# Strassen blocks with 512-column passes over both halves of the input, modulation sums stacked before one turn

## The chip, the cores and the metric

The kernel runs on one core of a Trainium2 chip. The metric is the time of one execution on the device in microseconds. The engines are named as the profile names them: PE (TensorE, its weight loads as PEld), DVE (VectorE), ACT (ScalarE), POOL (GpSimd) and SP (SyncE, which issues most transfers).

## The reference

Two transformer blocks in float32 on 512 tokens of width 1024. What this change touches is the feed-forward part of each block and the modulation of the second one:

```
h = rmsnorm(x, ...)                              # (512, 1024)
y = (silu(h @ w_gate) * (h @ w_up)) @ w_down     # hidden width 2816, once in each block

mod = silu(c) @ mod_w + mod_b                    # c (1, 1024), mod_w (1024, 6144), second block only
shift1, scale1, gate1, shift2, scale2, gate2 = split(mod, 6)
```

## The kernel before

Every large product is computed in three passes of fp32r matmuls. Weight and input are split into a high part (ACT casts it) and a low part (DVE subtracts), and PE adds hi x hi, hi x lo and lo x hi in PSUM. A unit of weights is 1024 rows by 256 columns (or 512 by 512) and is loaded by SP into one of two `raw` slots; the slots of `w_hi` and `w_lo` alternate too. PSUM is `bank`, 8 banks of 512 columns.

**Up stage.** There are two of them (`hidden` on ACT and DVE, `blocks` on POOL and PE), with `which` 0 and 1. The first 4 of 22 units are plain. The other 18 are *blocks* m = 0 to 17: one block holds the same 128 columns of gate and up, and is computed by a Strassen scheme with 7 products of a quarter of the weights (4 k-tiles of 128 rows) and 256 tokens, 12 matmuls of 256 columns each. PE takes them in the order P7, P6, P4 of block m, P1 of block m+1, P5 of m, P2 of m+1, P3 of m (`pe_order`, and the loop at L2437). P1, P6, P5 and P3 add up in one region "x"; P2, P7 and P4 have a region each, half a bank wide (`region`, L628).

Around the products, block m needs on DVE, in this order: `pair_lo` of m+1 (L1748), the product of m-1 (L1814), `b22_lo` (L1771, its end lets SP load the weights of block m+2), two sums of weight quarters of m+1, t1 and t3 (L1735, L1741), z = P6 + P7 (L1831), c21 = z - P4 (L1834), `sums_lo` of m+1 (L1757), c22 (L1840), `t4_lo` and `t1_lo` of m+1 (L1764 twice), the last product (L1845), and the sum with P2 of m+1 (L1820). POOL makes t2 (L987, after t1) and t4 (L991, after t2) of block m+1. ACT casts the high parts and copies P7 (L1264) and P1 (L1233) out of PSUM. `sums_lo` reads t2, so it waits for POOL; PE waits for c22 of m before P3 of m, and for `sums_lo` of m+1 before P7 of m+1. Each engine runs its list strictly in order; all waits are on counters whose values follow from these lists (`dve_order`, `act_order`, `wait_pool`).

**Modulation.** For the four early pairs of 1024 columns, DVE multiplies slabs of `mod_w` with silu(c) and adds them, over 128 partitions (`early_slab`), into one of two accumulators. For each pair PE then turns the accumulator with 8 transposes (`mod_columns`, L2589) and DVE sums the turned columns (L1702): twice in the k stage and twice in the va stage. The gate of the last norm is spread over the partitions by 4 matmuls (`mod_gate` on PE, L2596 and L2597) in the second down stage; its high part is cast by ACT (`mod_hi_part(5)`) in that stage, and its low part is made by POOL (`mod_lo_part(5)`, L1052) after the last block.

Of the kernel before, what the change touches and what calls it, by code (L numbers as in the profile page):

```python
# [31 lines left out]
F32 = mybir.dt.float32  # L32
# [5 lines left out]
P = 128  # L38
# [105 lines left out]
def build(nc, a, out):  # L144
    with ExitStack() as ctx:
# [15 lines left out]
        h_hi = at("h_hi", 48, [P, KD, TOK], F32R)  # L161
        h_lo = at("h_lo", 64, [P, KD, TOK], F32R)
# [42 lines left out]
        s_hi = at("s_hi", A + 12, [P, 4, 4, 256], F32R)  # L205
        s_lo = at("s_lo", A + 28, [P, 4, 4, 256], F32R)
# [249 lines left out]
        class Chain:  # L456
# [46 lines left out]
        GAINS_READY, GATE_READY = {1: 5, 2: 7}, {2: 8, 3: 9}  # L503
# [158 lines left out]
        def dve_order():  # L662
# [3 lines left out]
            for m in range(BLOCKS):  # L666
# [6 lines left out]
                yield from [f"sums {ahead}"] if ahead else []  # L673
                yield f"c22 {m}"
                yield from [f"t4 {ahead}", f"t1_lo {ahead}"] if ahead else []
# [24 lines left out]
        def wait_pool(eng, which, m, total):  # L700


            eng.wait_ge(block_pool, 2 * BLOCKS * which + 2 * m + total)
# [178 lines left out]
        def _(gp):  # L882
# [54 lines left out]
            def early_pairs():  # L937

                for e, pair in enumerate(EARLY):
                    acc, col = mod_both[e % 2], 512 * MOD_PAIRS[pair][0]  # L940
                    wait(gp, mod_read, e - 1)
# [13 lines left out]
            def mod_pair(pair):  # L955

                place = LATER.index(pair)
                wait(gp, mod_read, len(EARLY) + place)
# [20 lines left out]

            def blocks(n0, which):  # L980

                for m in range(BLOCKS):
# [8 lines left out]
                    gp.tensor_tensor(t4, t2, quarter_of(n, 1, 0), ALU.subtract).then_inc(block_pool, 1)  # L991

# [4 lines left out]
            gp.wait_ge(mod_read, 3)  # L997
# [72 lines left out]
        def _(act):  # L1070
# [48 lines left out]
            def post_norm(k, n0, units, xn, gain, shift):  # L1119
# [6 lines left out]
                for j in range(units):  # L1126
# [4 lines left out]
                    if k == 3 and j == 1:  # L1131
                        mod_hi_part(5)
# [1814 lines left out]
```

## Time and profile before

| | |
|---|---|
| median of 3 runs (lowest, highest) | 1534.05 us (1533.6, 1534.14) |
| the profiled execution's own time | 1534.35 us |
| its span, from the first to the last instruction | 1532.6 us |
| granted clock of TensorE over the span | 0.999 of 2.4 GHz |
| first up stage, blocks 0 to 17 | from 471.15 to 654.07 us |
| second up stage, blocks 0 to 17 | from 1222.28 to 1405.20 us |
| share of the chain that ended last | PE 96%, DVE 2%, ACT 1% |

A matmul's duration in the profile holds its way through the array, and matmuls overlap; what one costs in a stream is the distance between two starts. The same holds, less strongly, for DVE and ACT, where the next instruction starts a little before the one ahead has ended.

### The profile page before, as it was taken

The numbers are of one execution on the slowest core, as the hardware profiler recorded it, in microseconds if no ns is written. First come the engines' busy times: TensorE is split into PE (matmuls) and PEld (weight loads), VectorE is DVE, ScalarE is ACT, GpSimd is POOL, SyncE is SP. The second block draws the span as 40 slices with busy tenths as digits, with TensorE's granted clock in tenths as the row PEclk, the third lists the DMA queues.
The fourth block names the chain that finished last, engine by engine and source line by source line (L and its number), as shares of the span: only waits on it lengthen the run. The fifth ranks groups of instructions, "written<-read, shape, count | busy, mean of one in ns | idle before, by whom it ended". The sixth has DMA issues, their size and how long they took to land.

```text
span 1532.6 us, 23103 instructions
## 1 busy us (share of the span) xinstructions
PE 1521.0 (99%) x8916; PEld 1340.0 (87%) x8916; DVE 989.4 (65%) x1427; ACT 675.3 (44%) x1109; POOL 386.5 (25%) x350
## 2 busy tenths in 40 slices
PE   9999999999999999999999999999999999999998
PEld 9888887888899999988898888888888999999886
DVE  4776667547588777773276979644456977777323
ACT  5223444423454544442186775332226554455221
POOL 3211004210112222396010802692012122222000
PEclk9999999999999999999999999999999999999999
DMA  7875113322432444354222211453232233334231
GB/s 214 301 256 165 56 55 69 111 83 83 137 108 59 110 111 110 114 189 144 91 84 69 83 55 57 136 154 114 90 101 65 83 110 106 93 106 143 91 110 55
DMA packets 188726, 171.41 MB, mean 112 GB/s; under 512 B 19793, under 2 KB 161105, under 8 KB 188625
## 3 DMA queue, kind: packets, MB, share of 16 engines
q1 hardware_dynamic: 181456, 144.84, 31.5%
q0 software_dynamic: 7168, 25.19, 5.0%
q8 instruction: 68, 1.11, 0.3%
q14 instruction: 34, 0.27, 0.1%
HBM read 167.91 MB, written 2.10 MB: 111 GB/s over the span
## 4 chain that ended last, share of the span: by engine, by line
PE 96%; DVE 2%; ACT 1%; issue 0%; POOL 0%; DMA 0%; SPq 0%; DVEq 0%; ACTq 0%; POOLq 0%
PE bank L2321 19%; PE bank L2323 19%; PE bank L2322 19%; PE bank L2415 7%; PE bank L2417 7%; PE bank L2416 7%; PE bank L2480 2%; PE bank L2481 2%; PE bank L2484 2%; PE bank L2644 1%; PE bank L2376 1%; PE bank L2389 1%; PE bank L2385 1%; PE bank L2543 1%; PE bank L2655 1%
## 5 line engine op out<-in xcount | busy, mean ns | idle before, releaser
L1572 DVE TENSOR_TENSOR w_lo<-raw,w_hi 128x2048 fp32r<-128x2048 f32 (+1 forms) x109 | 213.3, 1958 | 216.9 <-ACT w_hi L1082 216.6
L2321 PE MATMUL bank<-h_hi,w_hi 128*128 128x512 f32 (+1 forms) x800 | 308.9, 386 | 0.0
L2323 PE MATMUL bank<-h_hi,w_lo 128*128 128x512 f32 (+1 forms) x800 | 298.5, 373 | 0.0
L2322 PE MATMUL bank<-h_lo,w_hi 128*128 128x512 f32 (+1 forms) x800 | 298.2, 373 | 0.0
L1082 ACT CAST w_hi<-raw 128x2048 fp32r<-128x2048 f32 (+1 forms) x108 | 171.5, 1588 | 200.1 <-PE bank L2323 194.1
L2321 PEld LDWEIGHTS bank<-h_hi,w_hi 128*128 128x128 f32 x800 | 150.9, 189 | 28.5 <-issue 1.9
L2322 PEld LDWEIGHTS bank<-h_lo,w_hi 128*128 128x128 f32 x800 | 151.0, 189 | 27.0 <-issue 1.9
L2323 PEld LDWEIGHTS bank<-h_hi,w_lo 128*128 128x128 f32 x800 | 150.7, 188 | 27.1
L2415 PE MATMUL bank<-s_hi,w_hi 128*128 128x256 f32 x576 | 163.4, 284 | 2.0 <-DVE act_m L1840 2.0
L2417 PE MATMUL bank<-s_hi,w_lo 128*128 128x256 f32 x576 | 163.0, 283 | 0.0
L2416 PE MATMUL bank<-s_lo,w_hi 128*128 128x256 f32 x576 | 163.0, 283 | 0.0
L987 POOL TENSOR_TENSOR w_sum<-raw,act_m 128x512 f32<-128x512 f32 x36 | 48.9, 1358 | 314.4 <-PE bank L2417 225.6
L2416 PE MATMUL bank<-h_lo,w_hi 128*128 128x256 f32 x432 | 122.3, 283 | 0.0
L2417 PE MATMUL bank<-h_hi,w_lo 128*128 128x256 f32 x432 | 122.2, 283 | 0.0
L2415 PE MATMUL bank<-h_hi,w_hi 128*128 128x256 f32 x432 | 122.2, 283 | 0.0
L2415 PEld LDWEIGHTS bank<-s_hi,w_hi 128*128 128x128 f32 x576 | 110.5, 192 | 2.8 <-DVE act_m L1840 2.8
L2416 PEld LDWEIGHTS bank<-s_lo,w_hi 128*128 128x128 f32 x576 | 110.6, 192 | 0.0
L2417 PEld LDWEIGHTS bank<-s_hi,w_lo 128*128 128x128 f32 x576 | 110.6, 192 | 0.0
L2321 PE MATMUL bank<-w_hi,act_hi 128*128 128x512 f32 x280 | 109.0, 389 | 0.0
L2323 PE MATMUL bank<-w_hi,act_lo 128*128 128x512 f32 x280 | 108.9, 389 | 0.0
L2322 PE MATMUL bank<-w_lo,act_hi 128*128 128x512 f32 x280 | 108.9, 389 | 0.0
L2415 PEld LDWEIGHTS bank<-h_hi,w_hi 128*128 128x128 f32 x432 | 82.9, 192 | 0.1
(489 smaller groups left out, 3217.8 us busy)
## 6 DMA issues: line engine op xcount, KB each, us to landing
raw<-in_w_in SPq DMA_DIRECT2D x102, 512.0 KB, 4.6
raw<-in_w_ffn_in SPq DMA_DIRECT2D x44, 512.0 KB, 5.1
mod_slabs<-in_mod_w POOLq DMA_DIRECT2D x16, 1024.0 KB, 6.0
raw<-in_w_gate SPq DMA_DIRECT2D x22, 512.0 KB, 4.0
raw<-in_w_up SPq DMA_DIRECT2D x22, 512.0 KB, 5.2
raw<-in_w_down SPq DMA_DIRECT2D x20, 512.0 KB, 4.6
raw<-in_w_ffn_out SPq DMA_DIRECT2D x20, 512.0 KB, 4.4
mod_raw<-in_mod_w POOLq DMA_DIRECT2D x32, 256.0 KB, 3.1
```

The costliest lines, as they stand in the source:

```text
L987: gp.tensor_tensor(t2, quarter_of(n, 1, 1), four(t1_sum(m)), ALU.subtract).then_inc(block_pool, 1)
L1082: ins = act.copy(w_hi[s][:, cols], raw[s][:, cols])
L1572: ins = dve.tensor_tensor(w_lo[s][:, cols], raw[s][:, cols], w_hi[s][:, cols].bitcast(F32), ALU.subtract)
L2321: pe.matmul(o, st_hi, mv_hi, start=first, stop=False)
L2322: pe.matmul(o, st_hi, mv_lo, start=False, stop=False)
L2323: return pe.matmul(o, st_lo, mv_hi, start=False, stop=last)
L2415: pe.matmul(o, hi[:, k, :], mv_hi(k), start=first and k == 0, stop=False, skip_group_check=not first)
L2416: pe.matmul(o, hi[:, k, :], mv_lo(k), start=False, stop=False, skip_group_check=not first)
L2417: ins = pe.matmul(o, lo[:, k, :], mv_hi(k), start=False, stop=k == 3, skip_group_check=not first)
L2480: pe.matmul(bank[:, t, 0:width], x_hi[:, k0 + k, ts], hi[:, k, :], start=first and k == 0, stop=False)
L2481: pe.matmul(bank[:, t, 0:width], x_lo[:, k0 + k, ts], hi[:, k, :], start=False, stop=False)
L2484: ins = pe.matmul(bank[:, t, 0:width], x_hi[:, k0 + k, ts], lo[:, k, :], start=False, stop=last and k == kt - 1)
```

## The change

P2, P7 and P4 no longer run hi x hi and hi x lo as two matmuls of 256 columns. The high and low parts of the input lie in one tensor (`h_parts`, `s_parts`), and one matmul of 512 columns takes both (two stretches of 256, 16 KB apart); its results lie side by side in one bank, hi x lo in the second half (`both_parts`). Lo x hi stays a matmul of 256 columns into the first half. All 8 banks are used, 4 for even and 4 for odd blocks. The second halves are added afterwards: those of P2 and P4 by one more DVE instruction each (L1856 and L1869 of the changed kernel), that of P7 by ACT, which copies both halves, and POOL, which adds them (L1009); z waits for POOL.

The products on PE:

```diff
                     for k in range(4):
+                        parts = moving(k)
+                        if name == "x":
+                            pe.matmul(o, hi[:, k, :], parts[:, 0, :], start=first and k == 0, stop=False, skip_group_check=not first)
+                            pe.matmul(o, hi[:, k, :], parts[:, 1, :], start=False, stop=False, skip_group_check=not first)
+                        else:
+                            pe.matmul(both_parts(m, name), hi[:, k, :], parts, start=k == 0, stop=k == 3, skip_group_check=True)
+                        ins = pe.matmul(o, lo[:, k, :], parts[:, 0, :], start=False, stop=k == 3,
+                                        skip_group_check=not first or name != "x")
```

ACT's copies of P7, and behind t2 and t4 of the same block POOL's sum:

```diff
-                    act.copy(act_m[:, PLAIN + m, 256:512], region(m, "p7")).then_inc(block_act, 1)
+                    act.copy(act_m[:, PLAIN + m, 256:512], region(m, "p7"))
+                    act.copy(act_m[:, PLAIN + m, 0:256], region(m, "p7", 1)).then_inc(block_act, 1)
...
+                    if which == 1 and m == 4:
+                        mod_lo_part(5)
+                    wait_act(gp, which, f"p7 {m}")
+                    p7, p7_second = act_m[:, PLAIN + m, 256:512], act_m[:, PLAIN + m, 0:256]
+                    gp.tensor_tensor(p7, p7, p7_second, ALU.add).then_inc(block_pool, 1)
```

DVE in block m:

```diff
-                    dve.tensor_tensor(g[:, 0:256], region(m, "p2"), g[:, 0:256], ALU.add)
+                    chain.mark(dve.tensor_tensor(g[:, 0:256], region(m, "p2"), g[:, 0:256], ALU.add))
                     if m + 1 < BLOCKS:
                         pair_lo(m + 1)
+                    chain.wait()
+                    dve.tensor_tensor(g[:, 0:256], region(m, "p2", 1), g[:, 0:256], ALU.add)
...
-                    wait_act(dve, which, f"p7 {m}")
+                    wait_pool(dve, which, m, 3)
...
-                    dve.tensor_tensor(g[:, 256:512], g[:, 256:512], region(m, "p4"), ALU.subtract).then_inc(block_dve, 1)
-                    if m + 1 < BLOCKS:
+                    then(dve.tensor_tensor(g[:, 256:512], g[:, 256:512], region(m, "p4"), ALU.subtract))
+                    dve.tensor_tensor(g[:, 256:512], g[:, 256:512], region(m, "p4", 1), ALU.subtract).then_inc(block_dve, 1)
+                    if 0 < m < BLOCKS - 1:
                         sums_lo(m + 1)
...
                     dve.tensor_tensor(mid[:, 256:512], region(m, "x"), mid[:, 256:512], ALU.add).then_inc(block_dve, 1)
+                    if m == 0:
+                        sums_lo(1)
```

In the first block c22 stands ahead of `sums_lo(1)`. In the last block PE has one set of transposes (first up stage) or the gate's 4 matmuls (second) between P5 and P3. ACT's cast for that gate moves into block 1 of the second stage and POOL's low part into block 4.

```diff
+                    else:
+                        wait_dve(pe, which, f"c21 {m}")
+                        if which == 0:
+                            mod_columns(0)
+                        else:
+                            mod_gate(5, 6)
                     wait_dve(pe, which, f"c22 {m}")
```

The four early accumulators are not turned one by one. DVE folds each from 128 to 32 partitions and stacks the four in `mod_acc`; PE turns the stack once, in the last block of the first up stage; DVE sums 32 columns at a time (`early_columns`, two reductions) after that stage.

```diff
+            def fold(e):
+                acc = mod_both[e % 2][:].rearrange("p a n -> p (a n)")
+                stack = mod_stack[:].rearrange("p a n -> p (a n)")
+                dve.wait_ge(mod_summed, SLABS * (e + 1))
+                then(dve.tensor_tensor(acc[0:64, :], acc[0:64, :], acc[64:128, :], ALU.add))
+                dve.tensor_tensor(stack[32 * e:32 * e + 32, :], acc[0:32, :], acc[32:64, :], ALU.add).then_inc(mod_out, 1)
...
-                mod_columns(i, (shift_col[0], gain_sums[0])[i])
+                fold(i)
```

How the lists of the engines change shows in three places. First DVE, one block in the middle of the first up stage, before (from `pair_lo` of m+1 on):

```order
L1748 TENSOR_TENSOR w_lo_53<-raw_50,w_hi_51 128x1024
L1814 TENSOR_TENSOR act_m<-bank,silu_t 128x256
L1771 TENSOR_TENSOR w_lo_54<-raw_49,w_hi_52 128x512
L1735 TENSOR_TENSOR act_m<-raw_50 128x512
L1741 TENSOR_TENSOR w_sum_87<-raw_50 128x512
L1831 TENSOR_TENSOR silu_t<-bank,act_m 128x256
L1834 TENSOR_TENSOR silu_t<-silu_t,bank 128x256
L1757 TENSOR_TENSOR w_lo_53<-w_sum_87,w_hi_51 128x1024
L1840 TENSOR_TENSOR act_m<-bank,act_m 128x256
```

The same stretch of DVE in the changed kernel (line numbers are its own):

```order
L1780 TENSOR_TENSOR w_lo_53<-raw_50,w_hi_51 128x1024
L1856 TENSOR_TENSOR silu_t<-bank,silu_t 128x256
L1846 TENSOR_TENSOR act_m<-bank,silu_t 128x256
L1803 TENSOR_TENSOR w_lo_54<-raw_49,w_hi_52 128x512
L1767 TENSOR_TENSOR act_m<-raw_50 128x512
L1773 TENSOR_TENSOR w_sum_86<-raw_50 128x512
L1865 TENSOR_TENSOR silu_t<-bank,act_m 128x256
L1868 TENSOR_TENSOR silu_t<-silu_t,bank 128x256
L1869 TENSOR_TENSOR silu_t<-silu_t,bank 128x256
L1789 TENSOR_TENSOR w_lo_53<-w_sum_86,w_hi_51 128x1024
L1875 TENSOR_TENSOR act_m<-bank,act_m 128x256
```

L1856 (second half of P2) stands ahead of the product and of `b22_lo`, L1869 (second half of P4) ahead of `sums_lo`; nothing has left the list.

POOL, before, the end of the second up stage (L987 is t2, L991 is t4):

```order
L991 TENSOR_TENSOR w_sum_87<-w_sum_88,raw_50 128x512
L987 TENSOR_TENSOR w_sum_88<-raw_49,act_m 128x512
L991 TENSOR_TENSOR w_sum_87<-w_sum_88,raw_49 128x512
L1052 TENSOR_TENSOR mod_lo<-mod_acc,mod_hi 128x1024
L895 TENSOR_SCALAR sq_y<-sq_y 128x1
```

POOL in the changed kernel, blocks 3 to 5 of the second up stage (L1000 is t2, L1004 is t4, L1009 the new sum of P7's halves, L991 the gate's low part):

```order
L1000 TENSOR_TENSOR w_sum_87<-raw_49,act_m 128x512
L1004 TENSOR_TENSOR w_sum_86<-w_sum_87,raw_49 128x512
L1009 TENSOR_TENSOR act_m<-act_m 128x256
L1000 TENSOR_TENSOR w_sum_87<-raw_50,act_m 128x512
L1004 TENSOR_TENSOR w_sum_86<-w_sum_87,raw_50 128x512
L991 TENSOR_TENSOR mod_lo<-mod_acc,mod_hi 128x1024
L1009 TENSOR_TENSOR act_m<-act_m 128x256
```

Every block's sum stands between t4 of this block and t2 of the next; the gate's low part, 1024 columns, has come forward from behind the last block to right behind t4 of block 4.

## Rows read from the trace of the kernel before

**Rows 1.** The page's part 1: busy us of each engine, share, instructions.
```profile
PE 1521.0 (99%) x8916; PEld 1340.0 (87%) x8916; DVE 989.4 (65%) x1427; ACT 675.3 (44%) x1109; POOL 386.5 (25%) x350
```

**Rows 2.** Waits of PE: line, releaser, total us, times, longest.
```profile
PE bank L2415 <- DVE act_m L1840: 2.0, 4, 0.6
```

**Rows 3.** Timeline of PE in the blocks: start, duration, line, operation, idle.
```profile
484.00 0.28 PE L2415 MATMUL bank<-s_hi,w_hi 128*128 128x256 f32 x1
...
490.49 0.28 PE L2415 MATMUL bank<-s_hi,w_hi 128*128 128x256 f32 x1
...
563.92 0.28 PE L2415 MATMUL bank<-s_hi,w_hi 128*128 128x256 f32 x1
```

**Rows 4.** Timeline of PE: the waits in the first and last block.
```profile
483.19 0.39 PE L2415 MATMUL bank<-s_hi,w_hi 128*128 128x256 f32 x1 [0.36 <-DVE act_m L1840]
...
652.54 0.39 PE L2415 MATMUL bank<-s_hi,w_hi 128*128 128x256 f32 x1 [0.62 <-DVE act_m L1840]
```

**Rows 5.** Timeline of PE: one set of columns, one gate, what follows.
```profile
101.99 1.04 PE L2589 MATMUL bank<-ident,mod_acc 128*128 128x128 f32 x8
102.78 0.47 PE L2576 MATMUL bank<-h_hi,wf_both 128*40 128x512 f32 x1
...
1443.31 0.39 PE L2596 MATMUL bank<-mod_hi,ones_r 128*128 128x512 f32 x1
...
1444.22 0.39 PE L2480 MATMUL bank<-w_hi,act_hi 128*128 128x512 f32 x1
```

**Rows 6.** Timeline of DVE, blocks 1 and 2 of the first stage.
```profile
477.59 0.69 DVE L1735 TENSOR_TENSOR act_m<-raw 128x512 f32<-128x512 f32 x1
...
484.59 0.42 DVE L1820 TENSOR_TENSOR silu_t<-bank,silu_t 128x256 f32<-128x256 f32 x1
485.34 1.23 DVE L1748 TENSOR_TENSOR w_lo<-raw,w_hi 128x1024 fp32r<-128x1024 f32 x1 [0.33 <-ACT w_hi L1201]
...
487.41 0.68 DVE L1735 TENSOR_TENSOR act_m<-raw 128x512 f32<-128x512 f32 x1
...
492.54 0.42 DVE L1840 TENSOR_TENSOR act_m<-bank,act_m 128x256 f32<-128x256 f32 x1
```

**Rows 7.** Timeline of DVE, a block in the middle.
```profile
557.28 0.69 DVE L1735 TENSOR_TENSOR act_m<-raw 128x512 f32<-128x512 f32 x1
...
561.31 1.22 DVE L1757 TENSOR_TENSOR w_lo<-w_sum,w_hi 128x1024 fp32r<-128x1024 f32 x1 [1.01 <-POOL w_sum L991]
562.68 0.43 DVE L1840 TENSOR_TENSOR act_m<-bank,act_m 128x256 f32<-128x256 f32 x1
```

**Rows 8.** Timeline of POOL.
```profile
23.45 0.21 POOL L912 TENSOR_TENSOR start_sel<-ident 128x8 fp32r<-128x8 f32 x1
...
478.35 1.68 POOL L987 TENSOR_TENSOR w_sum<-raw,act_m 128x512 f32<-128x512 f32 x1 [13.84 <-DVE act_m L1735]
...
558.48 1.29 POOL L987 TENSOR_TENSOR w_sum<-raw,act_m 128x512 f32<-128x512 f32 x1 [7.35 <-PE bank L2417]
559.91 1.30 POOL L991 TENSOR_TENSOR w_sum<-w_sum,raw 128x512 f32<-128x512 f32 x1
...
1135.12 2.40 POOL L1052 TENSOR_TENSOR mod_lo<-mod_acc,mod_hi 128x1024 fp32r<-128x1024 f32 x1 [89.17 <-ACT mod_hi L1117]
```

**Rows 9.** Timeline of DVE and POOL in the first down stage.
```profile
656.28 2.62 DVE L1572 TENSOR_TENSOR w_lo<-raw,w_hi 128x2048 fp32r<-128x2048 f32 x1
...
657.72 2.33 POOL L973 TENSOR_TENSOR mod_acc<-mod_acc,mod_raw 128x512 f32<-128x512 f32 x1
...
658.82 1.77 DVE L1714 TENSOR_TENSOR act_lo<-act_m,act_hi 128x512 fp32r<-128x512 f32 x1
```

**Rows 10.** Timeline of ACT.
```profile
484.25 1.05 ACT L1201 CAST w_hi<-raw 128x1024 fp32r<-128x1024 f32 x1 [1.27 <-DMA raw<-in_w_up]
...
556.92 0.37 ACT L1264 COPY act_m<-bank 128x256 f32<-128x256 f32 x1 [0.82 <-PE bank L2417]
...
1234.77 1.05 ACT L1201 CAST w_hi<-raw 128x1024 fp32r<-128x1024 f32 x1 [0.66 <-DMA raw<-in_w_ffn_in]
```

More of the change, by code:

```diff
@@ L672, in dve_order @@
                 yield f"c21 {m}"
-                yield from [f"sums {ahead}"] if ahead else []
+                yield from [f"sums {ahead}"] if ahead and m > 0 else []
                 yield f"c22 {m}"
+                yield from [f"sums {ahead}"] if m == 0 else []
                 yield from [f"t4 {ahead}", f"t1_lo {ahead}"] if ahead else []
@@ L957, in mod_pair @@
                 place = LATER.index(pair)
-                wait(gp, mod_read, len(EARLY) + place)
+                gp.wait_ge(mod_read, 1 + place)
                 then(gp.memset(mod_acc[:], 0.0))
@@ L1270, in hidden @@
                     act.activation(g, g, ACT.Silu).then_inc(block_act, 1)
+                    if which == 1 and m == 1:
+                        mod_hi_part(5)
                     if m + 1 < BLOCKS:
@@ L1910, in _ @@
             early_slab(12)
-            mod_columns(2, gain_sums[1])
+            fold(2)
             early_slab(13)
@@ L2408, in blocks, with product @@
             def blocks(n0, which):
-                def product(m, i, name, mv_hi, mv_lo, first=True):
+                def product(m, i, name, moving, first=True):
                     hi, lo, o = four(operand(w_hi, n0, i)), four(operand(w_lo, n0, i)), region(m, name)
                     for k in range(4):
-                        pe.matmul(o, hi[:, k, :], mv_hi(k), start=first and k == 0, stop=False, skip_group_check=not first)
-                        pe.matmul(o, hi[:, k, :], mv_lo(k), start=False, stop=False, skip_group_check=not first)
-                        ins = pe.matmul(o, lo[:, k, :], mv_hi(k), start=False, stop=k == 3, skip_group_check=not first)
+                        parts = moving(k)
[6 more added lines that the diff above has]
+                                        skip_group_check=not first or name != "x")
                     ins.then_inc(product_done, 1)
@@ L2580, in mod_columns @@
             def mod_columns(place):
-                early = place < len(EARLY)
-                acc = mod_both[place % 2] if early else mod_acc
-                pe.wait_ge(mod_summed, SLABS * (place + 1) if early else SLABS * len(EARLY) + 1)
-                wait(pe, mod_out, place if early else 0)
+                if place == 0:
+                    pe.wait_ge(mod_out, len(EARLY))
+                else:
+                    pe.wait_ge(mod_summed, SLABS * len(EARLY) + 1)
+                acc = (mod_stack, mod_acc)[place]
                 for q in range(KD):
@@ L2609, in _ @@
             f_pairs(n_q + 2, 1)
-            for i in range(2):
-                for j in range(2):
-                    for f in range(2):
-                        feature_tile(n_k + j, f, pair_pace(i))
-                mod_columns(i)
+            f_pairs(n_k, 2)
             pe.wait_ge(wf_split, 2)
@@ L2619, in _ @@
                 for j in range(2):
[L2620 to L2626 removed]
+                    token_unit(n_va + j, h_hi, h_lo, 4 * j, j == 0, j == 1, chunk_pace(c))
                     if c != j:
                         pe.wait_ge(rows_split, 1)
[L2629 removed]
                         for h in range(4 * c, 4 * c + 4):
```

117 lines of the change are left out of this document (58 added, 59 removed).

## The prediction

> **What bounds the kernel now.** The page's busy times come first: PE works 1521.0 of 1532.6 us, DVE two thirds of that [rows 1]. Then PE's waits: nearly the only ones it has in the up stages are four for c22 (L1840 of DVE), 2.0 us together [rows 2]. So in the blocks PE is the bound, and what a matmul costs there is the distance of starts: from 484.00 to 490.49 us lie 54 matmuls of 256 columns, 0.120 us each [rows 3]. For 512 columns the gate's four give (1444.22 - 1443.31) / 4 = 0.2275 us [rows 5]. A block of 84 matmuls takes 84 x 0.120 = 10.08 us. The third view asks how near the others are behind PE. In the middle of a stage c22 starts at 562.68 and lasts 0.43, and P3, which waits for it, starts at 563.92 [rows 3, 7]: it is ready 0.8 us early. The fourth view is the order of work: in a block DVE, then POOL, then DVE again make one ring, and this ring decides the case.
>
> **The ring, before.** t1 (DVE) -> t3 -> t2, t4 (POOL) -> `sums_lo` -> c22 -> `t4_lo`, `t1_lo` -> last product -> P2's sum -> `pair_lo` -> product -> `b22_lo` -> t1 of the next block. Where nothing but itself held it, at the start of the first stage, t1 starts at 477.59 and 487.41 [rows 6], 9.82 us. In it DVE stood still before `pair_lo`, whose weights came late [rows 10]: P2's sum starts at 484.59 and an instruction of this kind frees DVE after 0.33 (its 0.42 less the overlap), so 485.34 - 484.92 = 0.42 us. The ring by itself takes 9.40 us, 0.68 less than PE's block.
>
> **PE's saving.** In each block 3 products x 4 tiles lose one matmul: 2 x 0.120 - 0.2275 = 0.0129 us, 0.155 a block, 5.6 us for 36 blocks. PE's block falls to 9.93 us, if nothing else holds it. No row has a matmul that reads two stretches; the bounds are 0.2275 and 0.240 (two matmuls of 256), and I take the former. The Trainium skill (TensorE: Matmul & The Clock Gate, Back-to-back issue gap) gives an isolated gap of N / 2.4 + 2.5 ns. By it a removed matmul would save 2.5 ns, an estimate of 1.1 us in all; the rows' distances hold 13 ns above N / 2.4, so here the trace decides.
>
> **What is added to the ring.** First P2's second half (L1856 after), one more PSUM instruction of 256 columns: 0.33 us; it also stands ahead of `b22_lo`. Second POOL's sum of P7's halves. P4's second half (0.5 us with the wait for the first) falls into the 1.0 us that DVE waits for POOL before `sums_lo` [rows 7], and is free. POOL's instruction: 8 columns took 0.21, 1024 columns 2.40, 512 columns 1.29 [rows 8], a line of 0.19 + 2.16 ns a column, so 0.74 us for 256. Bounds: 0.65 (half of 1.29) and 1.29 (no faster than 512 columns); I take the line.
>
> When does it run? ACT's copy of P7 starts 0.2 us after P7's end (556.92 [rows 10]), takes 0.26 for each half, so POOL may start about 2.3 us after P7's start. DVE is then in `b22_lo`, with t1 and t3 right behind. All three read two SBUF operands, and there the trace shows that DVE and POOL keep each other out. t2 at 478.35, begun while t3 ran, took 1.68 us, and 1.29 at 558.48 when t3 had just ended [rows 8]. In the down stage a POOL sum begun at 657.72, in the middle of a DVE subtraction, took 2.33 instead of 1.29, and DVE's next one, from 658.82, took 1.77 instead of 0.69, ending 0.54 after POOL's [rows 9]. So at the end of a DVE instruction the waiting POOL gets in, and DVE waits until 0.15 us before POOL's end. This is what the Trainium skill states (SBUF — State Buffer, SBUF: two separate sides): one port pair is shared as an exclusive lock, for a DVE instruction with two SBUF inputs against a GpSimd instruction that reads SBUF; the trace agrees. Hence POOL's sum holds t1 up by 0.74 - 0.15 = 0.59, less what it can overlap with the end of `b22_lo`: 0.52. The sum lies ahead of t2 in POOL's list, so running it later moves t2 instead, with the same effect.
>
> The ring after: 9.40 + 0.33 + 0.52 = 10.25 us. It is longer than PE's 9.93 and than the 10.08 of before. PE will wait for c22 before every P3, some 0.2 to 0.3 us, and a block takes 0.17 us more than before. From block 2 to block 16 that is 15 x 0.17 = 2.5 us a stage.
>
> **The ends of the stages.** First block: c22 no longer waits for `sums_lo(1)`, so the waits at 483.19 (0.36 idle by the row, 0.6 from start to start) go in both stages [rows 4]. But in block 1 c22 comes late: before it ended at 492.54 + 0.42 = 492.96 with P3 due at 483.19 + 10.08 = 493.27. In the first stage its chain starts with the weights' arrival (ACT's cast at 484.25 waits for the transfer [rows 10]); the transfer starts 0.33 later, since `b22_lo` does, and another 0.33 comes from P2's second half: 493.62, so P3 is 0.4 us later than before, and a restart costs 0.1: +0.5. In the second stage the weights are there 0.6 us earlier (1234.77, as against 484.25 + 751.13, the distance of the two stages [rows 4, 10]): +0.0. Last block: PE's 0.8 to 0.9 us before P3 (idle 0.62 in the row [rows 4]) are filled with the transposes or the gate, but c22 comes later by P4's second half, about +0.4 each.
>
> **POOL's gate part, second stage.** It lasts 2.40 us [rows 8], stands right behind t4 of block 4, and reads two SBUF operands. Without a wait POOL starts its next instruction at once, while `sums_lo(4)` starts 0.1 us after t4's end (559.91 + 1.30, then 561.31 [rows 7, 8]). So POOL gets the port, `sums_lo(4)` and c22(3) are 2.2 us late, and with the ring now the bound PE gets none of it back. ACT's 1.05 us cast, now in block 1, delays `t4_lo(2)` by some 0.4 more. Together +2.6. If DVE gets the port first, it is about +0.9 in place of 2.6.
>
> **Outside the blocks.** One set of transposes costs 102.78 - 101.99 = 0.79 us; four go from the k and va stages, -3.2, the one that comes back is in the last block's wait. The gate's 4 matmuls go from the down stage, -0.9 [rows 5]. DVE's folds (8 instructions of 1024 columns) replace eight reductions there, a microsecond more for each pair; PE waits nowhere in these stages, a third of DVE is idle in the whole, and I cost them at 0. Were that cover gone, each would cost 1.2 us. `early_columns` (two reductions) lies beside the 5.4 us of the first down unit: 0.
>
> **Sum.** First stage 0.5 + 2.5 + 0.4 = 3.4; second 0.0 + 2.5 + 0.4 + 2.6 = 5.5; outside -4.1. Together +4.8 us on the profiled execution's 1534.35: 1539.15. That execution is 0.3 above the median shown, so 1538.9 is expected, and I say 1539. Its own range, from POOL's 0.65 (a ring of 10.16, -2.7) and the gate's part behind DVE (-1.7) up to 0.85 (+3.5), is 1534.5 to 1542.5.
>
> **Rivals.** The first rival: PE stays the bound and the change gains. If the port is not fought over, or POOL's sum gets in during P2's second half and the product, which read PSUM, the ring is 9.73, below 9.93. Then PE's -5.6 counts, the first waits go (-1.2), 0.6 comes back in block 1 of the first stage, and the last block keeps its +0.4 in each stage: -5.4, and with -4.1 outside 1524.8. For it: c22's 0.8 us of room. Against it: rows 8 and 9, and POOL's start at 2.3 us falls into `b22_lo`.
>
> The second: about nothing. The ring is as computed but DVE gets the port ahead of the gate's part and POOL's sum takes 0.65: +4.8 - 1.7 - 2.7 = +0.4, 1534.5. Half of it gives 1536.6, also within 0.2%.
>
> The third: clearly slower. The same ring with POOL's sum at 1.04, halfway to the upper bound: +0.3 a block, 34 blocks, +10: 1549. At 1.29 it would be +19. The point from which the ring costs anything is a sum that holds DVE for more than 0.2 us.
>
> The fourth: the change doesn't do what it says, and a matmul over two stretches costs 0.240. Then PE's 9.93 is 10.08, still under the ring: the forecast stands, only rival 1 loses 5.6 and lands at 1530.4.
>
> **Numbers.** Forecast 0.47, rival 1 0.25, rival 2 0.20, rival 3 0.08. What a measurement here can tell from no change is 0.2%, 3.1 us. Slower holds the forecast and rival 3, less its lower edge: 0.52. Faster, below 1531, is rival 1: 0.25. Same: 0.23. The range must reach rival 1 and 1545 to leave out no more than 2 in 10: 1525 to 1545; the forecast's own stands above.
>
> **What would show it.** On DVE the distance of t1 to t1 in mid-stage is 10.25 against 10.08, with t1 (L1767) lasting 1.2 instead of 0.69, or POOL's sum (L1009) lasting over 1 us. PE shows a wait for c22 (L1875) in nearly every block, and one of 2.5 us in block 3 of the second stage. 512-column matmuls are 0.2275 apart. The k and va stages are 3.2 us shorter. The forecast is wrong if PE's block is under 10.0 us; then the sum found a free port.

## The result and the profile after

| | before | after |
|---|---|---|
| median (lowest, highest), same chip | 1533.89 us (1533.6, 1535.16), 6 runs | 1541.95 us (1541.59, 1542.7), 6 runs |
| the profiled execution's own time | 1534.35 us | 1542.14 us |
| first up stage, from P1(0) to the first down matmul | 182.92 us | 188.03 us |
| second up stage | 182.92 us | 190.63 us |

The ratio after to before is 1.0051, 95% interval 1.0041 to 1.0062. Slower by 8.1 us was measured and slower by 4.8 forecast: the case was right, the size was short by 3.3. The page of the kernel after, part 1, answers to [rows 1], and below it stands the first line of its part 4:

```profile
PE 1524.2 (99%) x8460; PEld 1315.0 (85%) x8460; DVE 1026.9 (67%) x1501; ACT 681.1 (44%) x1145; POOL 437.5 (28%) x386
...
PE 85%; DVE 7%; POOL 3%; ACT 1%; issue 1%; DMA 1%; SPq 0%; DVEq 0%; POOLq 0%; ACTq 0%
```

PE has 456 matmuls fewer and is busy for 3 us more: a matmul's row lasts 0.28 us or more and covers a short gap behind it. The share of the chain that DVE and POOL hold went from 2% to 10%: PE is no longer alone on the path. The waits of PE for c22, which were 2.0 us in four places [rows 2], say where (total, times, longest):

```profile
PE bank L2455 <- DVE act_m L1875: 6.4, 16, 2.5
```

PE's timeline of the kernel after gives the corners of the ledger: the first matmul behind the turned sums in attention (157.05 before), the start and end of the first up stage, and the same of the second.

```profile
153.21 0.59 PE L2359 MATMUL bank<-h_parts,w_hi 128*128 128x512 f32 x1
...
467.29 0.28 PE L2455 MATMUL bank<-h_parts,w_hi 128*128 128x256 f32 x1
...
655.32 0.40 PE L2529 MATMUL bank<-w_hi,act_hi 128*128 128x512 f32 x1
...
1223.29 0.28 PE L2455 MATMUL bank<-h_parts,w_hi 128*128 128x256 f32 x1
...
1413.92 0.40 PE L2529 MATMUL bank<-w_hi,act_hi 128*128 128x512 f32 x1
```

| part of the time | forecast | measured |
|---|---|---|
| ahead of the first up stage (471.15 became 467.29) | -3.2 | -3.9 |
| first up stage | +3.4 | +5.1 |
| between the stages (568.21 became 567.97) | 0 | -0.2 |
| second up stage | +5.5 | +7.7 |
| last down stage | -0.9 | -0.9 |
| sum | +4.8 | +7.8 |

Outside the stages the change does what it should, and a little more. The loss is all in the two up stages: the sum was 3.9 us short there and 0.9 too high outside, so that it missed by 3.0.

**A block in which POOL goes first.** DVE, then POOL, in the middle of the first stage. L1803 is `b22_lo`, L1767 t1, L1773 t3, L1009 POOL's sum of P7's halves, L1000 t2.

```profile
524.01 0.68 DVE L1803 TENSOR_TENSOR w_lo<-raw,w_hi 128x512 fp32r<-128x512 f32 x1
524.61 1.22 DVE L1767 TENSOR_TENSOR act_m<-raw 128x512 f32<-128x512 f32 x1
525.76 0.68 DVE L1773 TENSOR_TENSOR w_sum<-raw 128x512 f32<-128x512 f32 x1
...
524.37 0.92 POOL L1009 TENSOR_TENSOR act_m<-act_m 128x256 f32<-128x256 f32 x1 [5.60 <-ACT act_m L1275]
...
534.88 1.23 DVE L1767 TENSOR_TENSOR act_m<-raw 128x512 f32<-128x512 f32 x1
```

I take a row to start when its engine asks, with the wait for the port in its length. POOL asks 0.24 us before t1 starts. t1 takes 1.22 instead of 0.69 [rows 7], and from t1 to t1 it is 10.27 us. The forecast was 1.2 and 10.25.

**A block in which DVE goes first.** POOL asks at the same point, 0.24 us before t1, and does not get in:

```profile
628.33 2.13 POOL L1009 TENSOR_TENSOR act_m<-act_m 128x256 f32<-128x256 f32 x1 [5.60 <-ACT act_m L1275]
...
628.57 0.69 DVE L1767 TENSOR_TENSOR act_m<-raw 128x512 f32<-128x512 f32 x1
629.17 0.69 DVE L1773 TENSOR_TENSOR w_sum<-raw 128x512 f32<-128x512 f32 x1
630.49 0.42 DVE L1865 TENSOR_TENSOR silu_t<-bank,act_m 128x256 f32<-128x256 f32 x1 [0.63 <-POOL act_m L1009]
```

t1 and t3 go through undisturbed, POOL's sum lasts 2.13 us with the waiting in it, and now t2, behind it in POOL's list, and z on DVE are late. t1 follows 10.43 us later (639.00), 0.16 more. Ten of the 36 blocks go this way: POOL's sum lasts 2.13 or 2.14 us in six of the first stage and four of the second. In two of these ten something else came on top. One takes 10.76 us: the weights of the next `pair_lo` came late, since ACT's cast of them waited for its transfer. In the other, of 10.73 us and two blocks later, t4 waits for PE:

```profile
572.96 1.05 ACT L1211 CAST w_hi<-raw 128x1024 fp32r<-128x1024 f32 x1 [0.89 <-DMA raw<-in_w_up]
574.04 1.23 DVE L1780 TENSOR_TENSOR w_lo<-raw,w_hi 128x1024 fp32r<-128x1024 f32 x1 [0.25 <-ACT w_hi L1211]
...
590.31 1.30 POOL L1004 TENSOR_TENSOR w_sum<-w_sum,raw 128x512 f32<-128x512 f32 x1 [0.43 <-PE bank L2459]
```

**The gate's part.** POOL's t4 and `mod_lo` (L991), DVE's `sums_lo(4)` (L1789), and PE's P3 of block 3 (L2455), second stage:

```profile
1263.81 1.30 POOL L1004 TENSOR_TENSOR w_sum<-w_sum,raw 128x512 f32<-128x512 f32 x1
1265.07 2.38 POOL L991 TENSOR_TENSOR mod_lo<-mod_acc,mod_hi 128x1024 fp32r<-128x1024 f32 x1
...
1265.21 3.32 DVE L1789 TENSOR_TENSOR w_lo<-w_sum,w_hi 128x1024 fp32r<-128x1024 f32 x1 [1.45 <-POOL w_sum L1004]
...
1268.92 0.58 PE L2455 MATMUL bank<-s_parts,w_hi 128*128 128x256 f32 x1 [2.50 <-DVE act_m L1875]
1269.30 0.41 PE L2456 MATMUL bank<-s_parts,w_hi 128*128 128x256 f32 x1
1269.51 0.41 PE L2459 MATMUL bank<-s_parts,w_lo 128*128 128x256 f32 x1
```

POOL takes the port and `sums_lo` lasts 3.32 us instead of 1.23. PE stands still for 2.50 us, as forecast. The last rows were not forecast: behind the wait the matmuls of 256 columns are 0.21 us apart instead of 0.12, up to about 1272. Windows of the same trace say the same; the third figure from the end is the granted clock:

```profile
1223.29:1266.00 42.71, 41.85 (x296) 38.78 (x295) 35.17 (x60) 22.44 (x40) 15.89 (x13) 1.00 0.35 97
1266.00:1270.00 4.00, 1.50 (x8) 1.18 (x7) 4.00 (x5) 1.67 (x3) 1.45 (x1) 0.83 0.09 22
1270.00:1280.00 10.00, 10.00 (x67) 9.45 (x67) 7.74 (x15) 4.25 (x8) 3.42 (x3) 0.90 0.38 107
```

1.00 is 2.4 GHz; some 3 us from 1268.92 on ran at the lower level of 1.2 GHz.

### The profile page after: what moved, and what is told of

Its sections match the earlier page's. It is cut to its first block, busy times and chain, and to the rows that moved or that the text cites. A ratio compares the mean times of both kernels' runs of the same rounds, so it can differ in the third digit from the quotient of the medians.

```text
span 1540.4 us, 22310 instructions
## 1 busy us (share of the span) xinstructions
PE 1524.2 (99%) x8460; PEld 1315.0 (85%) x8460; DVE 1026.9 (67%) x1501; ACT 681.1 (44%) x1145; POOL 437.5 (28%) x386
## 3 DMA queue, kind: packets, MB, share of 16 engines
q8 instruction: 63, 1.03, 0.3%
## 4 chain that ended last, share of the span: by engine, by line
PE 85%; DVE 7%; POOL 3%; ACT 1%; issue 1%; DMA 1%; SPq 0%; DVEq 0%; POOLq 0%; ACTq 0%
PE bank L2359 19%; PE bank L2361 19%; PE bank L2360 19%; PE bank L2459 4%; PE bank L2458 3%; PE bank L2455 3%; PE bank L2456 2%; PE bank L2530 2%; PE bank L2529 2%; PE bank L2533 2%; DVE w_lo L1789 2%; POOL w_sum L1004 2%; POOL w_sum L1000 1%; PE bank L2680 1%; PE bank L2414 1%
## 5 line engine op out<-in xcount | busy, mean ns | idle before, releaser
L2359 PE MATMUL bank<-h_parts,w_hi 128*128 128x512 f32 (+1 forms) x800 | 309.0, 386 | 0.0
L2361 PE MATMUL bank<-h_parts,w_lo 128*128 128x512 f32 (+1 forms) x800 | 298.6, 373 | 0.0
L2360 PE MATMUL bank<-h_parts,w_hi 128*128 128x512 f32 (+1 forms) x800 | 298.3, 373 | 0.0
L2359 PEld LDWEIGHTS bank<-h_parts,w_hi 128*128 128x128 f32 x800 | 150.9, 189 | 28.4 <-issue 1.9
L2360 PEld LDWEIGHTS bank<-h_parts,w_hi 128*128 128x128 f32 x800 | 151.0, 189 | 27.0 <-issue 1.9
L2361 PEld LDWEIGHTS bank<-h_parts,w_lo 128*128 128x128 f32 x800 | 150.7, 188 | 27.1
L2459 PE MATMUL bank<-s_parts,w_lo 128*128 128x256 f32 x576 | 163.3, 284 | 0.0
L2455 PE MATMUL bank<-s_parts,w_hi 128*128 128x256 f32 x432 | 126.3, 292 | 6.8 <-DVE act_m L1875 6.4
L2456 PE MATMUL bank<-s_parts,w_hi 128*128 128x256 f32 x432 | 122.9, 285 | 0.0
L2459 PE MATMUL bank<-h_parts,w_lo 128*128 128x256 f32 x432 | 121.6, 282 | 0.0
L2459 PEld LDWEIGHTS bank<-s_parts,w_lo 128*128 128x128 f32 x576 | 110.3, 192 | 0.0
L1009 POOL TENSOR_TENSOR act_m<-act_m 128x256 f32<-128x256 f32 x36 | 45.1, 1253 | 214.6 <-ACT act_m L1275 214.6
L2458 PE MATMUL bank<-h_parts,w_hi 128*128 128x512 f32 x288 | 105.0, 399 | 0.0
L2455 PEld LDWEIGHTS bank<-s_parts,w_hi 128*128 128x128 f32 x432 | 82.6, 191 | 19.2 <-DVE act_m L1875 17.0
L2456 PEld LDWEIGHTS bank<-s_parts,w_hi 128*128 128x128 f32 x432 | 82.9, 192 | 0.0
L2459 PEld LDWEIGHTS bank<-h_parts,w_lo 128*128 128x128 f32 x432 | 82.1, 190 | 0.0
```

The lines of the kernel that those rows point to most:

```text
L1009: gp.tensor_tensor(p7, p7, p7_second, ALU.add).then_inc(block_pool, 1)
L2359: pe.matmul(o, st_hi, mv_hi, start=first, stop=False)
L2360: pe.matmul(o, st_hi, mv_lo, start=False, stop=False)
L2361: return pe.matmul(o, st_lo, mv_hi, start=False, stop=last)
L2455: pe.matmul(o, hi[:, k, :], parts[:, 0, :], start=first and k == 0, stop=False, skip_group_check=not first)
L2456: pe.matmul(o, hi[:, k, :], parts[:, 1, :], start=False, stop=False, skip_group_check=not first)
```

## The experiments

Theory: POOL's sum, which shares a port with DVE, and P2's second half have made the ring of DVE and POOL longer than PE's block. Rivals: the work of DVE as such; the filled gaps and the gate's part; what a wide pass itself costs. Ratios are to the kernel before on the same chip. "Stages" are the lengths of the two up stages in the profiled execution, one each: where an edit leaves a stage alone, its length can still differ by 0.6 (the first stage in experiment 5).

| kernel | median us | ratio (95% interval) | stages us |
|---|---|---|---|
| after | 1541.95 | 1.0051 (1.0041 to 1.0062) | 188.03, 190.63 |
| e_all_narrow | 1530.59 | 0.9975 (0.9963 to 0.9986) | 182.31, 184.23 |
| e_p7_narrow | 1530.08 | 0.997 (0.9958 to 0.9981) | 182.26, 184.39 |
| e_dve_p7 | 1531.49 | 0.9982 (0.9973 to 0.9991) | 182.35, 184.55 |
| e_p2_late | 1534.51 | 1.0 (0.9991 to 1.0009) | 184.14, 186.82 |
| e_gate_early | 1538.85 | 1.0028 (1.0019 to 1.0037) | 187.43, 187.01 |
| e_swap | 1535.87 | 1.0005 (0.9996 to 1.0014) | 184.05, 186.50 |
| e_half_sum | 1533.55 (one run) | none | 183.30, 186.30 |
| e_spacing | 1534.28 (one run) | none | 182.10, 185.63 |
| e_best2 | 1527.66 | 0.9957 (0.9943 to 0.9971) | 181.77, 181.77 |
| e_best3 | 1525.91 | 0.9943 (0.9929 to 0.9956) | 180.88, 180.86 |
| e_narrow_early | 1528.26 | 0.996 (0.9946 to 0.9973) | 182.31, 182.36 |

**1. All three products narrow again (e_all_narrow).**

> The changed kernel with all three products by passes of 256 columns again: stacking, filled gaps and the early gate part alone. Theory (the ring of DVE and POOL made the loss): the ring is 9.40 us again, TensorE's block 10.08 the bound. Against before: -5.0 outside the blocks (read from the two traces), -1.2 for the first waits, about +1.8 for the gate's part on POOL: 1529.5 us, and t1 to t1 10.08. Rival (the gaps and the gate's part on POOL carry the loss): at or above 1534.

```diff
-                        if name == "x":
+                        if name == "x" or name in ("p2", "p7", "p4"):
```

(and no second halves on ACT, DVE and POOL). 1530.6 us, against 1529.5 and 1534. c22 to c22 on DVE, its line is L1868 here:

```profile
549.15 0.42 DVE L1868 TENSOR_TENSOR act_m<-bank,act_m 128x256 f32<-128x256 f32 x1
559.24 0.42 DVE L1868 TENSOR_TENSOR act_m<-bank,act_m 128x256 f32<-128x256 f32 x1
```

10.09 us (10.08 in most blocks): PE's block of before. So stacking and filled gaps gain 0.25%, even with the gate's part in the stage, and the wide passes as built cost 11 us. The rival that blames the gaps is out.

**2. P7 alone narrow (e_p7_narrow).**

> The changed kernel with P7 alone by 256 columns again; P2 and P4 stay wide, and GpSimd's sum and ScalarE's second copy are gone. Theory: the ring is 9.40 + 0.33 = 9.73, below TensorE's block of 10.03 (8 wide tiles, 6 ns each saved by the changed kernel's rows), so TensorE is the bound and it takes 1529.5 us (1528 to 1531). Rival (P2's second half, or the work of DVE as such, is the cause): t1 to t1 stays above 10.08, 1535 or more.

The edit is that of 1 for "p7" alone; ACT's second copy and POOL's sum go with it. 1530.1 us, as the theory had it. P2's second half stays in, and the loss is gone: it takes both terms, or POOL's sum, to push the ring over PE's block.

**3. DVE adds P7's second block (e_dve_p7).**

> The changed kernel, all three products wide, but DVE adds P7's second block itself, straight from PSUM, behind t3, where it waits for GpSimd in any case. DVE has 36 instructions more, GpSimd 36 fewer. Theory (the shared port: GpSimd's sum holds t1 up): ring 9.73, TensorE's block 10.00 by the rows of the changed kernel: 1529 us (1527 to 1531). Rival (DVE's amount of work is the bound): DVE's block grows by 0.33 us, 1553.

```diff
-                    gp.tensor_tensor(p7, p7, p7_second, ALU.add).then_inc(block_pool, 1)
+                    then(dve.tensor_tensor(mid[:, 256:512], region(m, "p7", 1), mid[:, 256:512], ALU.add))
```

ACT's second copy of P7 goes too. 1531.5 us, 0.5 above the range that the theory gave, and far from the rival's 1553: DVE is busy for longer (1031.5 us instead of 1026.9) and the kernel is 10 us faster. It is where the addition stands and which port it reads through, not how much DVE has to do. PE's rate is now to be read, c22 at L1872:

```profile
1341.50 0.42 DVE L1872 TENSOR_TENSOR act_m<-bank,act_m 128x256 f32<-128x256 f32 x1
1351.50 0.42 DVE L1872 TENSOR_TENSOR act_m<-bank,act_m 128x256 f32<-128x256 f32 x1
```

10.00 us, not the 9.93 that I had worked out for PE. The wide passes give 0.08 x 16 = 1.3 us a stage, and yet the stages are no shorter than with narrow products. The later c22 in the last block, a wait for z in block 0 and, in the first stage, one for c22 at 509.77 take something back; what each takes I have not measured.

**4. P2's second half in DVE's wait (e_p2_late).**

> The changed kernel with P2's second half moved behind the first half of c21, where DVE waits for GpSimd; GpSimd's sum stays. Theory: the ring loses 0.33 us, 10.27 becomes 9.94, below TensorE's 10.00; only blocks in which GpSimd loses its turn at the port are longer (by about 0.1). About 9 us of the 13 gained in the stages go: 1533 us (1531 to 1535). Rival (P2's half was not in the ring): 1542 as before the move.

```diff
-                    chain.wait()
-                    dve.tensor_tensor(g[:, 0:256], region(m, "p2", 1), g[:, 0:256], ALU.add)
...
-                    then(dve.tensor_tensor(g[:, 256:512], g[:, 256:512], region(m, "p4"), ALU.subtract))
+                    chain.mark(dve.tensor_tensor(g[:, 256:512], g[:, 256:512], region(m, "p4"), ALU.subtract))
+                    dve.tensor_tensor(g[:, 0:256], region(m, "p2", 1), g[:, 0:256], ALU.add)
+                    chain.wait()
```

1534.5 us, in the range. 7.4 us come from moving one instruction of 0.33 us per block, so it was in the ring. In the second stage blocks take 10.00. In the first they take 10.09: there POOL asks just after t1 has started, and loses its turn in 13 of the 18 blocks.

```profile
554.10 0.69 DVE L1767 TENSOR_TENSOR act_m<-raw 128x512 f32<-128x512 f32 x1
...
554.17 1.80 POOL L1009 TENSOR_TENSOR act_m<-act_m 128x256 f32<-128x256 f32 x1 [5.59 <-ACT act_m L1275]
```

9.94 + 0.15 for the lost turn = 10.09.

**5. The gate's part ahead of the stage (e_gate_early).**

> The changed kernel with the gate's part of the second stage (ScalarE's cast and GpSimd's subtraction of 1024 columns) done ahead of the up stage, while the merge's down units run; the gate itself stays in the last block. Theory (this part takes the port ahead of sums_lo(4)): the wait of 2.50 us in block 3 of the second stage goes, and so does the slow stretch of TensorE behind it; the second stage comes down from 190.6 to about the 188.0 of the first: 1539 us (1538 to 1539.5). Rival (the ring catches the delay up elsewhere, or the subtraction is in DVE's way there too): 1541 to 1543.

```diff
+            mod_lo_part(5)
             post_norm(2)
             blocks(n_up2, 1)
...
+                if k == 2:
+                    mod_hi_part(5)
```

(each taken away from blocks 4 and 1). 1538.9 us, as expected, 3.1 less than after; the second stage falls from 190.63 to 187.01, so the part had cost some 3.6 us. The first stage, which the edit leaves alone, reads 187.43 instead of 188.03: single executions tell the price to about half a microsecond.

**6. b22_lo and the product exchanged (e_swap).**

> The changed kernel with b22_lo and the product (L1803 and L1846 there) exchanged, so that GpSimd's request for P7's sum, 0.24 us ahead of t1, falls into an instruction of DVE that reads PSUM. Theory (port, and who is asked at its boundary): GpSimd gets in at once in every block, t1 is late by about 0.34 instead of 0.54, no sum lasts 2.1 us, the ring is 10.07: t1 to t1 10.07, and 1542 - 2 x (15 x 0.20 + 1) = 1535 us (1533 to 1537). Rival (the sum costs the ring its own length wherever it lies): 1541 to 1543.

```diff
-                    if m > 0:
-                        product_of(m - 1)
                     b22_lo(m)
+                    if m > 0:
+                        product_of(m - 1)
```

1535.9 us, in the range. The product (L1846) reads PSUM, and POOL gets in while it runs:

```profile
554.52 0.41 DVE L1846 TENSOR_TENSOR act_m<-bank,silu_t 128x256 f32<-128x256 f32 x1
554.86 1.03 DVE L1767 TENSOR_TENSOR act_m<-raw 128x512 f32<-128x512 f32 x1
...
554.60 0.74 POOL L1009 TENSOR_TENSOR act_m<-act_m 128x256 f32<-128x256 f32 x1 [5.59 <-ACT act_m L1275]
```

t1 is late by 0.34 instead of 0.54, POOL's sum takes its bare 0.74 us in nearly all blocks, no turn is lost, and c22 to c22 is 10.07 or 10.08. Two instructions of the same engine, exchanged, are worth 6 us. This is rival 1's picture, half fulfilled: the sum runs beside an instruction that reads PSUM.

**7. Half of POOL's sum (e_half_sum).** The second 128 columns of P7's sum are left out.

> The changed kernel, GpSimd's sum over the first 128 of P7's 256 columns alone (the other 128 are left out). Theory (the lock lasts as long as GpSimd's instruction): the sum takes 0.19 + 2.16 ns x 128 = 0.47 us where nothing is in its way, t1 in the blocks in which GpSimd goes first takes 0.96 instead of 1.23, the ring is 10.00: 1534 us (1533 to 1537). Rival (a fixed cost of handing the port over): t1 stays 1.2, 1541 or more.

```profile
523.96 0.95 DVE L1767 TENSOR_TENSOR act_m<-raw 128x512 f32<-128x512 f32 x1
...
523.70 0.65 POOL L1009 TENSOR_TENSOR act_m<-act_m 128x128 f32<-128x128 f32 x1 [5.59 <-ACT act_m L1275]
```

t1 takes 0.95 where 0.96 was expected, blocks take 10.00. Without waiting the sum of 128 columns takes 0.46 us, of 256 columns 0.73. The lock lasts as long as POOL's instruction; there is no large fixed price in handing it over. 10.00 is PE's own block too, so the 10.00 alone would not show how short the ring has become: t1's length does.

**8. What a wide pass costs (e_spacing).** P7 is another product here, since its pass reads h_hi alone.

> The kernel in which DVE adds P7's second block, with each wide product in another form: P7's pass reads one stretch of 512 columns (h_hi's, in place of the sums' hi and lo, so P7 is another product), P2 is unchanged (two stretches of 256, passes of 512 and 256 in turn), P4 issues its four passes of 512 first and then the four of 256. TensorE is the bound here, so distances of starts can be read. Theory A (a pass over two stretches costs more): P7's passes 0.2275 us apart from what follows, P2's and P4's 0.2355. Theory B (the change of width between neighbours costs): P4's 0.2275, P7's and P2's 0.2355. By either it saves 0.03 us per product and block: 1530.5 us, no difference from 1531.5 that one look can tell.

```diff
+                    if name == "p4":
+                        for k in range(4):
+                            pe.matmul(both_parts(m, name), hi[:, k, :], moving(k), start=k == 0, stop=k == 3, ...)
+                        for k in range(4):
+                            ins = pe.matmul(o, lo[:, k, :], moving(k)[:, 0, :], start=False, stop=k == 3, ...)
...
+                            if name == "p7":
+                                parts = h_parts[:, 0, k, :].rearrange("p (a n) -> p a n", n=256)
```

PE's timeline, P4 with its passes grouped (L2451, L2453) and the start of what follows, then the first matmul of P7 with one stretch (L2464) and the first behind it:

```profile
1330.61 1.09 PE L2451 MATMUL bank<-h_parts,w_hi 128*128 128x512 f32 x4
1331.54 0.63 PE L2453 MATMUL bank<-h_parts,w_lo 128*128 128x256 f32 x4
...
1332.01 0.28 PE L2459 MATMUL bank<-h_parts,w_hi 128*128 128x256 f32 x1
...
1337.73 0.40 PE L2464 MATMUL bank<-h_parts,w_hi 128*128 128x512 f32 x1
...
1339.15 0.28 PE L2459 MATMUL bank<-s_parts,w_hi 128*128 128x256 f32 x1
```

P7 with one stretch takes 1.42 us, P2 unchanged 1.41 to 1.42, P4 grouped 1.40 in every block; three passes of 256 take 1.44. Theory A, that two stretches cost, is refuted. Theory B, that a neighbour of another width costs, holds in part: a change from 512 to 256 columns costs about 8 ns, four of them in turn 0.03 us, one 0.01. The time of this one run lies 3.8 us above the expected 1530.5. 2.8 us of it were there before the first stage began, which the edit does not touch. The second stage lasted 185.63 us instead of 184.55; behind the gate's part the granted clock fell to 0.51 here (1265 to 1268) and stayed at 1.00 in experiment 3. So the time says nothing of the passes.

**9. A better version, and what the wide passes are worth (e_best2, e_best3, e_narrow_early).**

> All three products wide; DVE adds P7's second block behind t3, and both halves of P2 stand beside z and c21, in DVE's wait for GpSimd; the gate's part of the second stage is done ahead of the stage. Theory (ring 9.40 - 0.33 = 9.07, TensorE's block of 10.00 is the bound in every block): against the kernel with DVE's addition alone (1531.5) the second stage loses its wait of 2.2 us and the single late blocks in both go (about 0.5 each): 1528.5 us (1527 to 1530). Rival (TensorE's block of 10.00 is not reached, since DVE with 10% more work is late in other places): 1531 or more.

> The kernel before this one, with each wide product's four passes of 512 columns ahead of its four of 256. From the rows of the spacing experiment a product so ordered takes 1.40 us instead of 1.42: 0.06 a block, 2.2 us in 36 blocks: 1526.5 us (1525 to 1528.5). Rival (the weights of the product's later tiles are not ready so early, or the 0.02 us are lost at the next neighbour): no difference from the kernel before this one.

> What the wide passes are worth once they are out of the ring: all three products by passes of 256 columns, with stacking, filled gaps and the gate's part of the second stage done ahead of the stage. Theory: TensorE's block is 10.08 instead of 9.94, 0.14 x 34 = 4.8 us more than in the kernel with grouped wide passes, less about 0.8 us at the two stage ends, where P4's second half makes c22 late: 1529.5 us (1528.5 to 1530.5), and 1 to 2 below the same kernel with the gate's part inside the stage (1530.6). Rival (the wide passes bring nothing): 1526.

e_best2 is edits 3 and 5, and both halves of P2 taken from the ring:

```diff
+                    chain.mark(dve.tensor_tensor(mid[:, 256:512], region(m, "p7", 1), mid[:, 256:512], ALU.add))
+                    chain.mark(dve.tensor_tensor(g[:, 0:256], region(m, "p2"), g[:, 0:256], ALU.add))
+                    chain.wait()
                     wait_product(dve, which, f"p6 {m}")
```

with the second half between the two of P4, as in 4. e_best3 adds the grouped passes of 8 for all three products, e_narrow_early is e_all_narrow with edit 5. They took 1527.7, 1525.9 and 1528.3 us: the first two as expected, the third 0.2 below its range. e_best3 is 0.57% faster than before and 16 us faster than the change as made. Its first line of part 4 and its c22 in two blocks:

```profile
PE 96%; DVE 2%; ACT 1%; issue 0%; DMA 0%; SPq 0%; POOL 0%; DVEq 0%; ACTq 0%
...
1326.79 0.42 DVE L1872 TENSOR_TENSOR act_m<-bank,act_m 128x256 f32<-128x256 f32 x1
1336.73 0.42 DVE L1872 TENSOR_TENSOR act_m<-bank,act_m 128x256 f32<-128x256 f32 x1
```

9.94 us a block, and PE waits for c22 in the last block of each stage alone. Against e_narrow_early both stages are shorter by 1.4 and 1.5 us: this is the whole worth of the wide passes, 2.9 us in the two stages. 0.14 x 17 = 2.4 us a stage are won in the blocks, so about 0.9 must be lost at the ends.

## Why the prediction was right, and where its size was off

**What bounds it.** Right. PE was the bound, and the ring of DVE and POOL took its place. t1 to t1 is 10.27 us where nothing else disturbs it, 0.02 beside the 10.25 of the sum; both terms added to the ring were shown by themselves: P2's 0.33 us (experiment 4), POOL's sum by its length and by its place (6, 7), and by its absence (3). The forecast wait for c22 in nearly every block is there: the view counts 16, and in 15 more blocks P3 starts 0.28 to 0.42 us after the matmul ahead of it, where 0.12 is usual and experiment 3 shows no such gap from 1290 to 1390.

**POOL's sum.** Right in length (0.74 by the line, 0.73 and 0.74 measured) and in what it does to t1 (0.52 forecast, 0.54 measured). The two rows of the kernel before that showed DVE and POOL keeping each other out [rows 9] were enough to size it. The Trainium skill (SBUF — State Buffer, SBUF: two separate sides) states that the shared port pair is an exclusive lock, held for the whole instruction. Experiments 6 and 7 agree: beside a DVE instruction that reads PSUM the sum ran in its bare 0.74 us, and a sum shorter by 0.27 us held t1 up by 0.27 less.

**The step that was short: "running it later moves t2 instead, with the same effect".** It does not have the same effect. POOL's requests fall some 0.25 us before t1 in 24 of the 36 blocks, and 10 of these lose. A lost turn costs 0.15 us more than a won one, since POOL waits for t1 and t3 both: 1.5 us in all, which the forecast did not have.

**A term that the forecast did not have: late weights.** From P3(1) to P3(16) the first stage took 4.6 us more than before, and the forecast had 2.5. The ring of 10.27 makes 15 x 0.19 = 2.9 of it and six lost turns 0.9. The other 0.9 stand beside two late transfers: ACT's casts at 500.58 and 572.96 waited 1.03 and 0.89 us for theirs, which made two blocks 0.2 and 0.4 us longer, and behind the second a block is 0.3 longer in which t4 waits for PE, late itself. The kernel before has such waits as well (0.99 us at 634.86), but there the ring was 0.68 us shorter than PE's block, and they cost nothing.

**The gate's part.** Its wait was right to a tenth (2.50 us, forecast: about 2.5), and so were the two terms of its price. `sums_lo(4)` took 2.1 us longer (forecast 2.2), and ACT's cast for the gate, 1.04 us from 1243.88 in block 1, stood ahead of the one that `t4_lo(2)` needs, so that DVE was 0.4 us late (forecast 0.4):

```profile
1245.73 0.69 DVE L1796 TENSOR_TENSOR w_lo<-w_sum,w_hi 128x512 fp32r<-128x512 f32 x1 [0.31 <-ACT w_hi L1225]
...
1249.41 1.22 DVE L1803 TENSOR_TENSOR w_lo<-raw,w_hi 128x512 fp32r<-128x512 f32 x1
...
1258.32 1.23 DVE L1780 TENSOR_TENSOR w_lo<-raw,w_hi 128x1024 fp32r<-128x1024 f32 x1 [0.34 <-ACT w_hi L1211]
```

But the part's price was some 3.6 us (experiment 5) and not 2.6. The forecast lacked two things. With DVE late, POOL's sum got in ahead of `b22_lo` (L1803, 1.22 us instead of 0.68) and not behind it. The end of `b22_lo` lets the next weights load: ACT's cast of them started 6.6 us after it, here as in experiment 5, and DVE waited for it at 1258.32, which made block 3 longer by 0.4. And there is the stretch at 1.2 GHz behind the wait: 11 matmuls that cost 0.09 us more each and two dearer ones, 1.4 us on PE. It made blocks 4 and 5 longer by 0.9 together; PE has no wait for c22 in them, and with the exchange of experiment 6, where PE stood still for 2.47 us and the clock stayed at 1.00, both blocks take that kernel's usual 10.07. In the whole, 15 blocks of the second stage took 7.2 us more than before: 2.9 by the ring, 0.6 by four lost turns, 2.1 and 0.4 by the two terms forecast, 0.4 by the late weights and 0.9 by the clock, each rounded.

**The ends.** Here the forecast was lucky in part: block 1 of the first stage was to cost +0.5, and it cost nothing, which hid as much of what was lacking elsewhere. P3(1) stands 22.19 us after the stage's start, 22.22 before. I had the transfer start later; it landed sooner (ACT's cast waited 0.46 us for it, not 1.27), and POOL's sum ran there beside P2's second half and the product. The last blocks cost 0.5 each, 0.4 was forecast.

**PE's saving.** The 5.6 us did not enter the forecast, since the ring hid them, but rival 1's number rested on them, and they were twice too large: 0.08 us a block, 2.9 in 36. 0.2275 us is the distance between passes of 512 columns among their like. Between passes of 256 columns it is 0.2355, the mean of 432 in the kernel of experiment 3, as in these rows of the kernel after:

```profile
535.14 0.41 PE L2458 MATMUL bank<-h_parts,w_hi 128*128 128x512 f32 x1
535.38 0.28 PE L2459 MATMUL bank<-h_parts,w_lo 128*128 128x256 f32 x1
535.50 0.39 PE L2458 MATMUL bank<-h_parts,w_hi 128*128 128x512 f32 x1
535.73 0.28 PE L2459 MATMUL bank<-h_parts,w_lo 128*128 128x256 f32 x1
```

Thus a wide tile takes 0.354 us, where three narrow passes take 0.360 and I had reckoned 0.3475; a block takes 10.00 and not 9.93. The fourth rival's bound of 0.240 was the nearer one. Rival 1 with its cause put right (experiment 3) came to 1531.5, by its own reckoning to 1524.8 or, with 0.240, 1530.4.

**Outside.** -4.1 was forecast, -5.0 measured. The four sets of transposes gave 3.8 us by the attention stage's start instead of 3.2. Part of this is the single execution: of the eleven kernels of the experiments, ten reach that point 2.8 to 4.0 us earlier than the kernel before, and e_spacing 1.1.

## What to carry to other kernels

An instruction that is moved to an idle engine is not free when that engine shares a port with the busy one: price it by its length on the ring that both form, and look at what the other engine does at the moment of the request. Move the work into the time in which the waiting engine waits for the other, and prefer there the instructions that read PSUM. And a saving on the bound engine is worth no more than the distance to the next bound: here 0.08 us a block on PE were bought with 0.87 us on the ring.

## What the hardware showed that I had not expected

- **A port's turn is not decided by the time of the request alone.** In 24 blocks of the kernel after POOL asked between 0.33 and 0.36 us after the start of `b22_lo`, as the rows have it; in 14 of them it got in at its end, in 10 it had to let t1 and t3 pass. With the request 0.07 us after t1's start (experiment 4) it let both pass each time, with the request 0.34 after t1's start (second stage there) it got in at t1's end each time. What decides is open.
- **The clock after a short wait.** After 2.50 us of standing still, behind 42 us at 2.4 GHz, PE ran at 1.2 GHz for some 3 us. The length of the wait does not decide it alone. In e_half_sum PE stood still for 2.21 us and the granted clock fell to 0.50 (1264 to 1267), in e_spacing for 1.99 us and it fell to 0.51; in e_dve_p7 after 2.22 us and in e_swap after 2.47 us it stayed at 1.00. The rows behind the wait in e_half_sum, e_swap and e_dve_p7, and a window of the last:

```profile
1263.71 0.58 PE L2455 MATMUL bank<-s_parts,w_hi 128*128 128x256 f32 x1 [2.21 <-DVE act_m L1875]
...
1265.33 0.39 PE L2455 MATMUL bank<-s_parts,w_hi 128*128 128x256 f32 x1 [2.47 <-DVE act_m L1875]
...
1262.54 0.39 PE L2452 MATMUL bank<-s_parts,w_hi 128*128 128x256 f32 x1 [2.22 <-DVE act_m L1872]
...
1260.00:1266.00 6.00, 3.78 (x27) 3.28 (x26) 6.00 (x9) 2.21 (x4) 1.06 (x1) 1.00 0.03 6
```

So such a fall is possible and not certain, and what decides is open; where it comes, a wait of two or three microseconds in a stream can cost half as much again (1.4 us on PE behind 2.50).
- **A change of width costs.** 512 columns among their like are 0.2275 us apart, 256 among theirs 0.120, and in turn the pair takes 0.354. Four and four, grouped, take 1.40 instead of 1.42 us, and 36 x 3 such products gave 1.8 us (e_best2 to e_best3).
